# A one-layer encoder block on one core: input LayerNorm in two pairs of tiles, unit transposes ahead of the first tile, zero writes later in the queue

## What is computed

```
h     = layernorm(x, ln0_w, ln0_b)                  # the input LayerNorm
proj  = h @ w_in                                    # q | k | v | z | xBC | dt | gates, 5136 columns
mix   = (sig(gA) * (attention(q,k,v) @ w_out_attn) + sig(gS) * (ssd(xBC, z, dt) @ w_out_ssd)) @ w_out
h1    = layernorm(alpha * h + mix)
out   = layernorm(alpha * h1 + moe(h1) + sig(h1 @ w_ple_gate + b) * (p @ w_ple))
```

## Time and profile before

| | |
|---|---|
| median of 3 runs | 796.5 us (796.02 to 796.9) |
| the profiled execution | 796.83 us, its span 795.0 us |
| TensorE busy (matmul) | 736.1 us, 93% of the span |
| VectorE busy | 422.8 us, 53% |
| ScalarE busy | 201.2 us, 25% |
| GpSimd busy | 183.9 us, 23% |
| DMA | 173.16 MB, mean 218 GB/s |

### The profile page before, as it was taken

The page is one execution under the profiler, slowest core; times in us unless marked ns, Lnnn a source line. Parts: engine busy times, 40 slices in busy tenths (PEclk is TensorE's granted clock), DMA queues, the critical chain, the costliest instruction groups (busy, mean ns, idle before and its releaser), DMA issues.

```text
span 795.0 us, 9744 instructions
## 1 busy us (share of the span) xinstructions
PE 736.1 (93%) x3799; PEld 519.1 (65%) x3799; DVE 422.8 (53%) x751; ACT 201.2 (25%) x351; POOL 183.9 (23%) x129
## 2 busy tenths in 40 slices
PE   4999999999999999999999999999999989888672
PEld 2897788998887878747888888544544444343220
DVE  6698946775678898663276947511221111021326
ACT  3312424555322323242130240211211111111130
POOL 4924490000032222004060002411111111111242
PEclk9999999999999999999999968999999999999985
DMA  9798132311121122324152496599999999999492
GB/s 308 268 409 196 53 107 60 101 54 54 44 65 54 54 54 54 132 106 158 54 229 90 168 403 223 171 418 419 409 412 418 420 421 419 420 420 415 144 204 107
DMA packets 61816, 173.16 MB, mean 218 GB/s; under 512 B 16982, under 2 KB 39712, under 8 KB 47946
## 3 DMA queue, kind: packets, MB, share of 16 engines
q1 hardware_dynamic: 52324, 141.79, 47.4%
q0 software_dynamic: 8752, 28.59, 11.1%
q10 hardware_dynamic: 694, 2.14, 0.7%
HBM read 155.52 MB, written 24.67 MB: 227 GB/s over the span
## 4 chain that ended last, share of the span: by engine, by line
PE 75%; DMA 11%; DVE 9%; issue 2%; POOL 1%; ACT 1%; SPq 0%; DVEq 0%; POOLq 0%
PE psum L902 34%; PE psum L1252 12%; PE psum L1190 6%; DMA ring<-in_w_exp_up_dram 6%; PE psum L1267 5%; PE psum L1111 3%; DMA ring<-in_w_in_dram 3%; PE psum L1060 2%; PE psum L1080 1%; PE psum L1193 1%; PE psum L1209 1%; PE psum L1010 1%; DMA arena<-y_rows,rowsU 1%; DVE arena L1676 1%; PE psum L979 1%
## 5 line engine op out<-in xcount | busy, mean ns | idle before, releaser
L902 PE MATMUL psum<-ring_r 128*128 128x512 f32 (+1 forms) x928 | 246.6, 350 | 4.1 <-DVE arena_r L1701 1.7
L902 PEld LDWEIGHTS psum<-ring_r 128*128 128x128 f32 x928 | 163.3, 191 | 29.0 <-issue 4.0
L902 PE MATMUL psum<-arena_r,ring_r 128*128 128x512 f32 (+1 forms) x416 | 140.9, 376 | 0.0
L751 POOL TENSOR_TENSOR ring_r<-ring,ring_r 128x2048 fp32r<-128x2048 f32 x16 | 73.8, 4619 | 204.6 <-ACT ring_r L1365 204.6
L1252 PE MATMUL psum<-ring,arena 128*64 128x512 f32 x512 | 114.6, 600 | 4.3 <-DMA ring<-in_w_exp_up_dram 4.3
L1365 ACT COPY arena<-psum 128x512 f32<-128x512 f32 (+4 forms) x104 | 57.3, 581 | 193.9 <-PE psum L1267 56.0
L1252 PEld LDWEIGHTS psum<-ring,arena 128*64 128x64 f32 x512 | 40.0, 138 | 76.2 <-issue 76.2
L902 PEld LDWEIGHTS psum<-arena_r,ring_r 128*128 128x128 f32 x416 | 79.2, 190 | 13.7 <-issue 0.5
L1267 PE MATMUL psum<-ring,arena 128*64 128x512 f32 x256 | 61.0, 619 | 9.2 <-issue 9.2
L1190 PE MATMUL psum<-arena 128*128 128x256 f32 x256 | 65.4, 403 | 1.2 <-DVE rowsU L2133 1.2
L2164 DVE SCALAR_TENSOR_TENSOR arena<-arena,psum 128x256 f32<-128x256 f32 x16 | 9.7, 609 | 105.0 <-ACT arena L1578 105.0
(11 more groups left out here) (299 smaller groups left out, 987.5 us busy)
## 6 DMA issues: line engine op xcount, KB each, us to landing
ring<-in_w_exp_up_dram SPq DMA_DIRECT2D x32, 1024.0 KB, 14.7
ring<-in_w_exp_down_dram SPq DMA_DIRECT2D x32, 1024.0 KB, 13.4
ring<-in_w_exp_gate_dram SPq DMA_DIRECT2D x32, 1024.0 KB, 12.7
ring<-in_w_in_dram SPq DMA_DIRECT2D x18, 1024.0 KB, 5.3
y_rows<-arena POOLq DMA_DIRECT2D x12, 1024.0 KB, 17.0
ring<-in_w_out_ssd_dram SPq DMA_DIRECT2D x4, 1024.0 KB, 7.1
ring<-in_w_out_dram SPq DMA_DIRECT2D x4, 1024.0 KB, 5.0
arena<-in_w_ple_gate_dram SPq DMA_DIRECT2D x4, 1024.0 KB, 15.8
```

Source lines behind the costliest of these rows:

```text
L751: g.tensor_tensor(lo, ring[:, SLOT_OF[seq]], hi.bitcast(F32), ALU.subtract).then_inc(s_w_lo, 1)
L902: t = mm(o, a, b, start=(first and j == 0), stop=(last and j == 2))
```

## The change

SyncE loads x tiles 0 and 1 ahead of the norm rows, and tiles 2 and 3 behind them. VectorE takes the statistics of tiles 0 and 1, their two roots, and normalises them; only after their `h_rest` does it take the statistics of tile 3 and the roots of tiles 2 and 3 (ScalarE does tile 2's statistics). ScalarE copies tiles 0 and 1 one behind the other and casts slices 1 and 2 after both. TensorE gets 14 transposes of the unit matrix, whose results nothing reads, ahead of tile 0's. GpSimd issues the twelve zero DMAs behind its subtraction for slice 3 instead of slice 1.

```diff
@@ sync
+            def x_rows(i):
+                sp.dma_start(h[:, i, :], x_v[:, i, :]).then_inc(x_in[i], 16)
+            x_rows(0)
+            x_rows(1)
             for j, name in enumerate(("ln0_w", "ln0_b")):
                 sp.dma_start(ln_rows[:, D * j:D * (j + 1)], aps[name].rearrange("(a n) -> a n", a=1)).then_inc(s_ln0_in, 16)
-            for i in range(NT):
-                sp.dma_start(h[:, i, :], x_v[:, i, :]).then_inc(x_in[i], 16)
+            x_rows(2)
+            x_rows(3)
@@ gpsimd
             for seq in range(2):
                 rest(seq)
-            zview_y = y_dram.rearrange("(p r) n -> p r n", p=P)
-            for r in range(0, zview_y.shape[1], 2):
-                pool.dma_start(zview_y[:, r:r + 2, :], zt).then_inc(s_zeroed, 16)
...
-            for seq in range(2, 8):
+            for seq in range(2, 4):
+                rest(seq)
+            zview_y = y_dram.rearrange("(p r) n -> p r n", p=P)
+            for r in range(0, zview_y.shape[1], 2):
+                pool.dma_start(zview_y[:, r:r + 2, :], zt).then_inc(s_zeroed, 16)
+            for seq in range(4, 8):
                 rest(seq)
@@ tensor
+            o = opened(("hT", 0, 0))
+            for _ in range(14):
+                tr(o[:, 0:P], ident, ident)
             h_turned(0)
             h_turned(1)
@@ scalar
-            act.wait_ge(x_in[1], 16)
-            tile_stats(h[:, 1, :], 1, sz[:, 1, :])
+            act.wait_ge(x_in[2], 16)
+            tile_stats(h[:, 2, :], 2, sz[:, 2, :])
...
+            part(0)
             for i in range(NT):
-                if i < 3:
-                    part(i)
+                if i == 2:
+                    part(1)
+                    part(2)
@@ vector
-            for i in (0, 2, 3):
+            def h_roots(tiles):
+                link(v.tensor_scalar(rv[0][:, tiles], mva[:, tiles, 1], LN_EPS, None, ALU.add))
+                rsqrt(rv[1][:, tiles], rv[0][:, tiles], rv[2][:, tiles])
+            for i in range(2):
                 dve.wait_ge(x_in[i], 16)
                 tile_stats(h[:, i, :], i)
-            dve.wait_ge(s_act_stats, 1)
-            link(v.tensor_scalar(rv[0], mva[:, :, 1], LN_EPS, None, ALU.add))
-            rsqrt(rv[1], rv[0], rv[2])
+            h_roots(slice(0, 2))
             dve.wait_ge(s_pe_ln0, 1)
             h_normed(0)
             h_normed(1)
             h_rest(0)
             h_rest(1)
+            dve.wait_ge(x_in[3], 16)
+            tile_stats(h[:, 3, :], 3)
+            dve.wait_ge(s_act_stats, 1)
+            h_roots(slice(2, NT))
             h_normed(2)
             h_normed(3)
             h_rest(2)
```

## The result

The changed kernel took **801.84 us** (median of 4 runs, 800.66 to 803.02), the kernel before 796.7 us on the same chip. The ratio is 1.006, with a 95% interval of 1.0046 to 1.0075: slower by some 5 us. The forecast was 800.4 in a range of 797.0 to 804.0. The profiled execution took 800.66 us, 3.83 more than the one of before (796.83), where the sum of the prediction had +3.9.

A forecast was written before the change was run, and what follows sets the result against it. VectorE's norm chain bounds the start, then TensorE, so a TensorE shift at 50 us moves the end equally. Late norms +3.3, clock +1.7, slice 4 -1.1 sum to +3.9: 800.4 us forecast, range 797.0 to 804.0.

The forecast's parts named there:

- When the first norm starts: VectorE's first norm, behind the spread of norm rows that queue behind x: starts at 13.8, a gain of 0.4 us.
- the rival in which they don't: Norm rows do not queue behind x: first norm at 10.9, sum +1.0, 797.5 us; chance 0.12.
- The 14 unit transposes: On TensorE ahead of tile 0's transposes: take 3.4 us at the low clock, standing 1.3 us in tile 0's way.
- GpSimd in the way: GpSimd's subtraction for slice 1 holds VectorE's roots until 27.25; third projection tile starts at 34.4: taken as +3.3 us.
- The clock: TensorE idles around tile 2's transposes, then runs at clock 0.57 for 4 us: +1.7 us, bounds 0 and twice that.
- Slice 4: With zero writes moved later, slice 4's load takes 5.4 us and TensorE's wait for it near 72 goes: -1.1 us.
- Slice 6 "cost nothing": Query weights' slice 6 meets the late zero writes: lands at 92.6, ready at 99.3, wanted near 103.9, so no cost.
- the rival's place: Zero writes delay slice 6 up to 10 us; GpSimd's scalings behind it hold VectorE's dt instructions: 2 to 6 us; chance 0.14.
- The sum: Whole kernel: 3.3 + 1.7 - 1.1 = +3.9 us, taking the profiled execution from 796.83 to 800.7.

The follow-up runs named there:

- the repeated execution: The changed kernel run once more, unaltered, beside others on one chip: 801.6 us (6 runs), ratio 1.0058 to the kernel before.

## Why the prediction was right, point by point

- **When the first norm starts.** Forecast 13.8, measured 13.35. The norm rows do queue behind x (6.06 where 6.6 was taken), and the rival in which they don't is refuted by the row at 6.06. Its world, made in the kernel with the norm rows first, gained 2.3 us where it was priced at 2.9: VectorE's first roots, behind x, came last there and not the spread.
- **The 14 unit transposes.** Forecast 3.4 us, measured 3.19, and tile 1 in 1.09: right. By "TensorE: Matmul & The Clock Gate", Part 1, of the Trainium skill the spread of one row alone should have lifted the clock; the 14 transposes directly behind it ran low here (3.19 us, 0.23 each), so the trace does not agree. The row of before that the prediction gave for this could not tell: 6.55 us of idle time lay between the spread and its transposes.
- **GpSimd in the way.** Roots until 29.05 forecast, 28.93 measured; GpSimd at 22.7 to 27.25, measured 22.27 to 26.90; third tile 34.4, measured 34.22. One detail was wrong: the prediction let the two root instructions with one input pass and held the third. The first was held. The end is nearly the same, since ten instructions of 0.2 us follow instead of nine. The trace of before could have told: its tensor_scalar at 116.02, with one input, was held for 4.04 us by GpSimd's run of two from 110.85. The sum had taken +3.3 for the third tile, for a clock that might still be low at tile 1; it was up, and the term measured +2.8.
- **The clock.** +1.7 forecast; 1.5 by the ledger, 1.6 by the kernel with 36 more transposes, and 0.6 more in the repeated execution.
- **Slice 4.** -1.1 forecast. The wait was there before and is gone after, and the ledger shows -1.4. But the term was given to the wrong part of the change: the shift of TensorE by 4.3 us takes that wait away by itself, as the kernel with the zero writes back shows. A sum of terms, each taken against the kernel before, can't tell that, and it hid that the zero move was worth next to nothing here.
- **Slice 6 "cost nothing".** Three of its four loads were issued at 65.0 to 67.0 and landed 24.4 to 26.0 us later, the last of them near the forecast 92.6. The fourth was issued only at 85.7, since the issue before it took SyncE 18.7 us, and landed at 94.1; that wait was not in the forecast. GpSimd was through with the slice at about 100.8 instead of 99.3, and TensorE still did not wait for it. The prediction had read the Trainium skill, "DMA: Bandwidth & Descriptors", Queues, rings and completion order, as bringing this slice sooner. The Trainium skill says there that an engine drains a packet of several descriptors before it switches; if the zeros' pieces come in such packets too, a turn of several pieces from each side gives the same landing as one of each, so these landings do not speak against it. The cost sat in what stands behind it on GpSimd, four scalings and a run of two subtractions, which hold VectorE's dt instructions: +0.6, the rival's place at a fraction of its price.
- **The sum.** +3.9 forecast, +3.83 between the profiled executions. That it agrees to 0.1 us is luck. The terms measured +2.8, +1.5, -1.4 and +0.6 where the sum had +3.3, +1.7, -1.1 and nothing, which is +3.5 up to the 64 matmuls; from there to the end the fourteen profiled executions took 459.8 to 463.8 us, and these two happened to differ by 0.3. The medians are 5.1 and 4.9 apart, 1 us more. Part of it is how long the low clock lasts behind the idle time (0.6 us between two executions of the same kernel), part lies behind 700 us, where the last gather of result rows took 9.29 us before, 9.19 with the change and 10.44 in its repetition (the rows `arena<-y_rows,rowsU` of their chains). Median less start of the 64 matmuls is 463.0 to 465.2 us in all fourteen, so 1 us is within the scatter of a single execution against its median; what is left of it stays open.

## What to carry to other kernels

When an instruction on VectorE moves, ask which GpSimd instruction it will now start beside: the first of eleven tiny instructions waited 4 us for its place, and one wait on GpSimd gave it back. Put the small loads that everything waits for ahead of the large ones. A transfer that is moved out of the way is worth what TensorE would have waited for it, which depends on all other edits: test it again in the kernel that it ends up in.

## What the runs showed of the hardware

- Size does not protect from the hold. Two elements a row waited 4.09 and 4.03 us, the whole rest of GpSimd's 4.6 us subtraction, and the instruction had only one input. The Trainium skill, "SBUF — State Buffer", section "SBUF: two separate sides", describes an exclusive lock that is kept for a whole instruction, and names VectorE instructions with two inputs in SBUF, beside a GpSimd one that reads SBUF, and those in a two-port mode as the ones that need it. That the lock is kept in full agrees with these rows; whether this tensor_scalar ran in such a mode no run here shows. The aggregate of the statistics, 0.21 us at 22.60 inside the same subtraction, and the norms with a PSUM input were not held.
- The clock did not rise the same way in each run of the same order. With the norm rows first and GpSimd's wait, tile 1's transposes took 1.97 us in one execution and 1.09 in another, both behind 14 unit transposes of 3.19 us. What decides between them stays open.
- A load in small pieces that is issued amid the zero writes ends some 5 us behind them, whenever it is issued. Slice 4 landed at 66.0 to 67.5 although its issue varied by 7.9 us, 40.66 to 48.58; the last zero write had landed at 61.0 to 63.6.
